# 104 overwritten products in front of one chunk pair: thirteen ways of reading the moving or the stationary side

## The chip, the core and the metric

The kernel runs on one core of one Trainium2 chip. The time is that of the device for one execution, in microseconds (us). The execution before has a median of 1122.11 us over two runs.

## What is computed

A row of 512 tokens with 1024 features goes through two blocks. The first has a gated spatial mix and a causal convolution, the second two kinds of attention. Each ends in a feed-forward part with 4096 hidden features. The pair in question belongs to that of the first block:

```python
h = rms_norm(x, norm2_g[l])
f = jnp.square(jax.nn.relu(jnp.einsum('bsd,df->bsf', h, w_ff1[l])))
x = x + jnp.einsum('bsf,fd->bsd', f, w_ff2[l])
```

All of it is float32 in the reference.

## The kernel before, in words

Activations lie transposed: a tile holds 128 features on the partitions and the 512 tokens along the free dimension. Each float32 matrix is split into a high part, rounded to a format that TensorE takes in one pass (`F32R` in the code, `fp32r` in the profile, though the profile writes a moving side of it as f32), and a low part, the rest. A product is made of three MATMULs: high x high, high x low, low x high (`three()`, lines 749 to 751). `xh` and `xl` are the high and low part of the normalised activations, of shape 128 x 8 x 512; `wh[slot]` and `wl[slot]` are those of a weight chunk of 128 x 1024 in one of four slots.

The weights come as a stream of chunks. Each chunk is loaded by DMA into `raw`, split by GpSimd (lines 548, 551 and 678 to 688 of the profile), and then used by TensorE.

The up-projection of a feed-forward part works on pairs of chunks, and in each pair it saves one product in eight: seven products of half size take the place of eight, with sums of weights and of activations as operands. The tokens are cut in two halves, `EARLY` (0 to 255) and `LATE` (256 to 511). `t_high[0..3]` and `t_low[0..3]`, each 128 x 4 x 256, hold the sums of activations, made once per feed-forward part. The weight sums are made per pair by VectorE (`weight_sums_first`, `weight_sums_last`, `weight_rest`) and ScalarE (`sum_round`). `pair(p)` issues the seven products of pair `p`. Each is a `product(...)`: four tiles of the contraction, three MATMULs of 256 columns each, 12 in all, so a pair is 84. `product_bank(p, i)` is the first half of one of the banks 0 to 4 in turn. VectorE adds the seven results into tiles and signals `part_added` and `evacuated`; ScalarE makes ReLU and square; then the next pair comes. TensorE waits for `split_ready` (GpSimd's split of the chunk), `sum_ready` (the weight sums), `part_added` and `evacuated` (a bank is free).

Four runs of pairs exist. Run 0 has pairs 0 to 3, run 1 pairs 4 to 11; `pairs_of(1)[2]` is pair 6, whose `place_in` is 2, and whose first product goes to bank (7 x 2 + 0) mod 5 = 4. The order on each engine is written out by hand and joined by semaphores. The slots are such that GpSimd splits the chunks of pair p + 1 after products of pair p (`split_pair` waits for `product_done`), and VectorE makes the weight sums of pair p + 1 while it adds the products of pair p.

Every `mm` (`nc.tensor.matmul`) is a load of the stationary side (LDWEIGHTS, engine PEld in the profile) and a MATMUL. `start=True` overwrites what the bank holds.

Of the kernel before, what the change touches and what calls it, by code (L numbers as in the profile page):

```python
# [32 lines left out]
P = 128  # L33
# [28 lines left out]
EARLY = slice(0, Q)  # L62
# [115 lines left out]
def pairs_of(run):  # L178

    first = sum(count for _, _, count in PAIR_RUNS[:run])  # L180
    return range(first, first + PAIR_RUNS[run][2])


def run_of(p):

    return next(run for run in range(len(PAIR_RUNS)) if p in pairs_of(run))


def place_in(p):

    return p - pairs_of(run_of(p))[0]
# [27 lines left out]
def build(nc, a):  # L219
    ctx = ExitStack()  # L220
    with ctx:
# [13 lines left out]
        def sem(name):  # L235
            return ctx.enter_context(nc.semaphore(name))
# [4 lines left out]
        xh = sb("xh", [P, KT, S], F32R)  # L241
# [4 lines left out]
        wh = [sb(f"wh{i}", [P, 1024], F32R) for i in range(SLOTS)]  # L246
        wl_at = place[0]
        wl = [sb(f"wl{i}", [P, 1024], F32R) for i in range(SLOTS)]
# [43 lines left out]
        half = FH // 2 * S * 4  # L292
# [33 lines left out]
        t_high = [at(f"t_high{i}", [P, 4, Q], F32R, o) for i, o in  # L326
                  enumerate((behind, behind + 8192, tmb_at, tmp_at))]
# [15 lines left out]
        bank = [ctx.enter_context(nc.psum_tensor(f"bank{i}", [P, S], F32)) for i in range(8)]  # L343
# [52 lines left out]
        product_done, product_kept, part_added = sem("product_done"), sem("product_kept"), sem("part_added")  # L396
# [348 lines left out]
        def _(pe):  # L745
            mm = nc.tensor.matmul
# [235 lines left out]
            for m in range(4):  # L982
                n = C_U + m
# [104 lines left out]
            def product(out, slot, part, mh, ml):  # L1088

                for k in range(4):  # L1090
                    ks = slice(512 * part + k * P, 512 * part + k * P + P)
                    last = three(out, wh[slot][:, ks], wl[slot][:, ks], mh(k), ml(k), k == 0, k == 3)
                return last

            def pair(p):

                n, run = chunk_of(p), run_of(p)
# [3 lines left out]
                slot = [slot_of(p, role) for role in range(4)]  # L1101

                pe.wait_ge(split_ready, n + 1)
                if alone:
                    pe.wait_ge(evacuated, e - 3)
                    if run == 3:
                        pe.wait_ge(down_out, 16 + TB + 1)
                else:
                    pe.wait_ge(part_added, 5 * p - 3)
                product(out[0], slot[0], 0, lambda k: xh[:, k, EARLY], lambda k: xl[:, k, EARLY]  # L1110
                        ).then_inc(product_done, 1)
                if alone:
# [1870 lines left out]
```

## Time and profile before

| What | Value |
|---|---|
| median of the runs | 1122.11 us |
| span of the profiled execution | 1120.9 us |
| instructions | 17261 |
| TensorE MATMUL busy | 1110.7 us, 6163 instructions |
| TensorE weight load busy | 940.3 us |
| VectorE busy | 704.8 us |
| GpSimd busy | 681.6 us |
| ScalarE busy | 401.7 us |

Times in the profile count from the start of the span. Busy time is the union of the instructions' durations on an engine. Durations of MATMULs overlap, since the next starts before the last has left the array; how fast a row of them goes is read from start to start. A line of the timeline with x4 is four instructions merged, with the time from the first start to the last end. PEclk is the granted clock of TensorE as a share of full speed (2.4 GHz).

### The profile page before, as it was taken

To read this page: it belongs to the slowest core of one execution; us is meant where nothing else is said; L and a number is where in the kernel's file an instruction comes from. 1 tells how busy PE (TensorE), PEld (TensorE's weight loads), DVE (VectorE), ACT (ScalarE), POOL (GpSimd) and SP (SyncE) were. 2 spreads that over 40 slices of the span, in tenths; PEclk is the share of its full clock that TensorE was granted. 3 is DMA by queue.
4 is the path that set the end of the run, shared out by engine and by line. 5 is a ranking of instruction groups with operands and counts; after the bars stand their busy time and mean duration, and the time that the engine had idled before them with its cause. 6 is when DMAs were issued, how large, how long until landed. Compare 5 with 4: busy or idle time off the path is not lost.

```text
span 1120.9 us, 17261 instructions
## 1 busy us (share of the span) xinstructions
PE 1110.7 (99%) x6163; PEld 940.3 (84%) x6163; DVE 704.8 (63%) x1381; ACT 401.7 (36%) x817; POOL 681.6 (61%) x460
## 2 busy tenths in 40 slices
PE   8999999999999999999999999999999999999997
PEld 6888888998889998888778777677899888999886
DVE  5999778850158853547789777666887113885023
ACT  5156566530015531120202346645665000554012
POOL 7879946586636686667456433135847763558662
PEclk9999999999999999999999999999999999999999
DMA  7321222342213342334343221112224822235412
GB/s 253 131 87 64 75 81 89 112 133 94 94 61 111 113 151 96 107 98 132 113 129 98 84 87 58 38 58 75 76 76 138 183 94 69 86 111 179 160 57 75
DMA packets 52251, 115.54 MB, mean 103 GB/s; under 512 B 21840, under 2 KB 22480, under 8 KB 52176
## 3 DMA queue, kind: packets, MB, share of 16 engines
q1 hardware_dynamic: 31200, 105.40, 28.3%
q10 hardware_dynamic: 20976, 9.15, 3.4%
q8 instruction: 46, 0.75, 0.3%
q14 instruction: 29, 0.24, 0.1%
HBM read 105.09 MB, written 4.19 MB: 97 GB/s over the span
## 4 chain that ended last, share of the span: by engine, by line
PE 96%; ACT 1%; DVE 1%; DMA 0%; issue 0%; SPq 0%; ACTq 0%; DVEq 0%
PE bank L749 21%; PE bank L751 20%; PE bank L750 20%; PE bank L1425 5%; PE bank L1427 5%; PE bank L1426 5%; PE bank L781 2%; PE bank L783 2%; PE bank L782 2%; PE bank L1260 2%; PE bank L822 1%; PE bank L1274 1%; PE bank L832 1%; PE bank L823 1%; PE bank L1214 1%; PE bank L1298 1%
## 5 line engine op out<-in xcount | busy, mean ns | idle before, releaser
L551 POOL TENSOR_TENSOR wl<-raw,wh 128x1024 fp32r<-128x1024 f32 x140 | 337.1, 2408 | 11.7
L548 POOL TENSOR_SCALAR wh<-raw 128x1024 fp32r<-128x1024 f32 x139 | 149.1, 1073 | 258.6 <-PE bank L751 144.0
L749 PE MATMUL bank<-xh,wh 128*128 128x512 f32 (+2 forms) x672 | 234.5, 349 | 0.0
L751 PE MATMUL bank<-xh,wl 128*128 128x512 f32 (+2 forms) x672 | 229.4, 341 | 0.0
L750 PE MATMUL bank<-xl,wh 128*128 128x512 f32 (+2 forms) x672 | 229.1, 341 | 0.0
L749 PEld LDWEIGHTS bank<-xh,wh 128*128 128x128 f32 x672 | 126.8, 189 | 29.1 <-issue 16.6
L1659 ACT ACTIVATE wh<-bank 128x512 fp32r<-128x512 f32 x96 | 52.2, 596 | 253.1 <-DVE bank L2338 109.7
L751 PEld LDWEIGHTS bank<-xh,wl 128*128 128x128 f32 x672 | 126.8, 189 | 14.2
L750 PEld LDWEIGHTS bank<-xl,wh 128*128 128x128 f32 x672 | 126.9, 189 | 12.6 <-issue 0.2
L749 PE MATMUL bank<-uh,wh 128*128 128x512 f32 x288 | 112.8, 392 | 0.0
L751 PE MATMUL bank<-uh,wl 128*128 128x512 f32 x288 | 112.1, 389 | 0.0
L750 PE MATMUL bank<-ul,wh 128*128 128x512 f32 x288 | 112.1, 389 | 0.0
L750 PE MATMUL bank<-t_low,wh 128*128 128x256 f32 x384 | 107.6, 280 | 0.0
L751 PE MATMUL bank<-t_high,wl 128*128 128x256 f32 x384 | 107.3, 280 | 0.0
L749 PE MATMUL bank<-t_high,wh 128*128 128x256 f32 x384 | 107.3, 279 | 0.0
L1426 PE MATMUL bank<-wl,uh 128*128 128x512 f32 x240 | 93.4, 389 | 0.0
L1427 PE MATMUL bank<-wh,ul 128*128 128x512 f32 x240 | 93.4, 389 | 0.0
L1425 PE MATMUL bank<-wh,uh 128*128 128x512 f32 x240 | 93.4, 389 | 0.0
L1986 DVE TENSOR_TENSOR bank<-bank,rb 128x512 f32<-128x512 f32 x16 | 11.2, 699 | 111.4 <-PE bank L751 111.4
L2353 DVE TENSOR_TENSOR wl<-bank,wh 128x512 fp32r<-128x512 f32 x96 | 63.2, 682 | 25.5 <-ACT wh L1659 25.0
L685 POOL TENSOR_SCALAR wh<-raw 128x512 fp32r<-128x512 f32 x24 | 14.9, 620 | 102.7 <-PE bank L751 90.0
L749 PEld LDWEIGHTS bank<-t_high,wh 128*128 128x128 f32 x384 | 72.8, 189 | 0.0
(378 smaller groups left out, 2283.2 us busy)
## 6 DMA issues: line engine op xcount, KB each, us to landing
raw<-wstream SPq DMA_DIRECT2D x188, 512.0 KB, 3.5
x<-xT SPq DMA_DIRECT2D x8, 256.0 KB, 4.8
x4rows<-x_rows ACTq DMA_DIRECT2D x4, 512.0 KB, 9.1
out<-x4rows SPq DMA_DIRECT2D x8, 256.0 KB, 2.1
qd<-ropey ACTq DMA_DIRECT2D x16, 64.0 KB, 2.2
kd<-ropey ACTq DMA_DIRECT2D x16, 64.0 KB, 2.1
qa<-ropey SPq DMA_DIRECT2D x16, 64.0 KB, 2.0
ka<-ropey SPq DMA_DIRECT2D x16, 64.0 KB, 2.0
```

Source lines behind the costliest of these rows:

```text
L548: nc.gpsimd.tensor_scalar(wh[c][:], raw[c][:], 1.0, 1.0, ALU.mult, ALU.mult).then_inc(high_ready, 1)
L551: nc.gpsimd.tensor_tensor(wl[c][:], raw[c][:], wh[c][:].bitcast(F32), ALU.subtract).then_inc(split_ready, 1)
L749: mm(out, wh_, mh, start=start, stop=False)
L750: mm(out, wh_, ml, start=False, stop=False)
L751: return mm(out, wl_, mh, start=False, stop=stop)
L781: mm(out, xh[:, k, ts], wh[s][:, ws], start=k == 0, stop=False)
L782: mm(out, xh[:, k, ts], wl[s][:, ws], start=False, stop=False)
L1425: mm(out, uh[:, f, ts], wh[s][:, ws], start=f == 0, stop=False)
L1426: mm(out, uh[:, f, ts], wl[s][:, ws], start=False, stop=False)
L1427: last = mm(out, ul[:, f, ts], wh[s][:, ws], start=False, stop=f == 15)
L1659: A(wh[slot_of(p, role)][:, 512 * part:512 * part + 512], bank[7 - made % 2][:], ACT.Copy).then_inc(sum_rounded, 1)
L2353: V.tensor_tensor(wl[slot][:, at], bank[7 - made % 2][:], wh[slot][:, at].bitcast(F32), ALU.subtract).then_inc(sum_ready, 1)
```

## The change

In front of pair 6, behind the waits of its first product, 104 MATMULs are issued. All write bank 4, each with `start=True` and `stop=True`, and nobody reads the results: product 0 of the pair starts afresh in the same bank. Thirteen ways of reading are gone through, each with k = 0 to 3 and the high and the low weights of the slot, which is eight MATMULs. Twelve ways differ in the moving side: `xh` or `t_high[0]` or `t_high[2]`, 128, 256, 384 or 512 columns, and either side by side or, with `turns(ap, n)`, in turn from n places (the innermost dimension has n elements, one from each n-th part of the tile). `half_tokens` takes 256 columns in turn from the two halves of 512 tokens, 0 to 127 and 256 to 383. The thirteenth reads `xh[:, k, 0:P]` as the moving side and every fourth element of `weights` as the stationary side.

```diff
--- before.py
+++ after.py
@@ -1107,6 +1107,30 @@
                         pe.wait_ge(down_out, 16 + TB + 1)
                 else:
                     pe.wait_ge(part_added, 5 * p - 3)
+                if p == pairs_of(1)[2]:
+                    pe.wait_ge(part_added, 5 * p - 3)
+                    whole = bank[(7 * place_in(p) + run // 3) % 5]
+
+                    def turns(ap, n):
+                        return ap.rearrange("p (half n) -> p n half", half=n)
+
+                    def half_tokens(ap):
+                        return ap.rearrange("p (half n) -> p n half", half=2)[:, 0:P]
+
+                    for moves in (lambda k: xh[:, k, EARLY], lambda k: turns(xh[:, k, EARLY], 2),
+                                  lambda k: half_tokens(xh[:, k]), lambda k: turns(xh[:, k, EARLY], 4),
+                                  lambda k: t_high[0][:, k], lambda k: turns(t_high[0][:, k], 2),
+                                  lambda k: turns(t_high[2][:, k], 2), lambda k: turns(xh[:, k], 2),
+                                  lambda k: turns(xh[:, k], 4), lambda k: turns(xh[:, k, P:], 2),
+                                  lambda k: xh[:, k, 0:P], lambda k: turns(xh[:, k, 0:P], 2)):
+                        for k in range(4):
+                            for weights in (wh[slot[0]], wl[slot[0]]):
+                                moved = moves(k)
+                                columns = int(np.prod(moved.shape[1:]))
+                                mm(whole[:, 0:columns], weights[:, k * P:k * P + P], moved, start=True, stop=True)
+                    for k in range(4):
+                        for weights in (wh[slot[0]], wl[slot[0]]):
+                            mm(whole[:, 0:P], weights[:, k:k + 4 * P:4], xh[:, k, 0:P], start=True, stop=True)
                 product(out[0], slot[0], 0, lambda k: xh[:, k, EARLY], lambda k: xl[:, k, EARLY]
                         ).then_inc(product_done, 1)
                 if alone:
```

## Rows read from the trace of the kernel before

**Rows 1.** The page: span, busy times of TensorE, its tenths, granted clock, chain.
```profile
span 1120.9 us, 17261 instructions
...
PE 1110.7 (99%) x6163; PEld 940.3 (84%) x6163; DVE 704.8 (63%) x1381; ACT 401.7 (36%) x817; POOL 681.6 (61%) x460
...
PEclk9999999999999999999999999999999999999999
...
PE 96%; ACT 1%; DVE 1%; DMA 0%; issue 0%; SPq 0%; ACTq 0%; DVEq 0%
```

**Rows 2.** Waits of TensorE, all; us in total, times, longest.
```profile
PE bank L969 <- DVE tmp L2040: 1.5, 1, 1.5
PE bank L945 <- DVE xl L2005: 1.0, 2, 0.5
PE bank L888 <- DVE rn L2034: 0.6, 1, 0.6
PE bank L822 <- issue: 0.2, 1, 0.2
```

**Rows 3.** Timeline of TensorE: first products of pairs 6 and 7, last of 5.
```profile
345.08 0.28 PE L751 MATMUL bank<-t_high,wl 128*128 128x256 f32 x1
345.19 0.28 PE L749 MATMUL bank<-xh,wh 128*128 128x256 f32 x1
...
355.10 0.28 PE L749 MATMUL bank<-xh,wh 128*128 128x256 f32 x1
```

**Rows 4.** Windows: span, busy of PE, PEld, DVE, ACT, POOL, clock, DMA, GB/s.
```profile
345.19:355.10 9.91, 9.91 (x86) 9.91 (x85) 8.72 (x18) 5.76 (x11) 5.98 (x5) 1.00 0.29 107
129.60:130.50 0.90, 0.90 (x4) 0.41 (x3) 0.69 (x2) 0.90 (x1) 0.90 (x1) 1.00 0.00 0
645.00:655.00 10.00, 10.00 (x60) 8.33 (x59) 6.58 (x23) 3.04 (x10) 3.43 (x2) 1.00 0.24 76
```

**Rows 5.** Waits of all engines in pair 6, the longest four.
```profile
ACT wh L1659 <- DVE bank L2345: 3.2, 1, 3.2
POOL wh L685 <- PE bank L751: 2.9, 1, 2.9
ACT wh L1659 <- DVE bank L2338: 0.9, 1, 0.9
POOL wh L678 <- PE bank L751: 0.9, 1, 0.9
...
```

**Rows 6.** Timeline of TensorE: steps of 512 and of 384 columns.
```profile
404.67 0.39 PE L749 MATMUL bank<-uh,wh 128*128 128x512 f32 x1
...
411.94 0.39 PE L751 MATMUL bank<-uh,wl 128*128 128x512 f32 x1
...
516.10 0.33 PE L749 MATMUL bank<-xh,wh 128*128 128x384 f32 x1
...
516.45 0.34 PE L751 MATMUL bank<-xh,wl 128*128 128x384 f32 x1
```

**Rows 7.** Timeline and groups of TensorE: plain f32 products, transposes, single columns.
```profile
129.61 1.02 PE L902 MATMUL bank<-conv_p,center 128*128 128x512 f32 x2
...
636.77 0.60 PE L1274 MATMUL bank<-ident,probs 128*128 128x128 f32 x4
...
647.26 1.03 PE L866 MATMUL bank<-inv,sq 128*128 128x1 f32 x8
...
L1274 PE MATMUL bank<-ident,probs 128*128 128x128 f32 x120 | 18.6, 274 | 0.0
...
L866 PE MATMUL bank<-inv,sq x32: 250/250/251, 647.3 to 694.7; 128*128 128x1 f32 x32
...
L902 PE MATMUL bank<-conv_p,center x2: 590/590/591, 129.6 to 130.0; 128*128 128x512 f32 x2
```

**Rows 8.** Groups of VectorE and GpSimd (line engine op names shapes xcount | busy us, mean ns).
```profile
L2344 DVE TENSOR_TENSOR bank<-raw,bank 128x512 f32<-128x512 f32 x24 | 16.5, 686 | 0.1
...
L551 POOL TENSOR_TENSOR wl<-raw,wh 128x1024 fp32r<-128x1024 f32 x140 | 337.1, 2408 | 11.7
```

## The prediction

> **What bounds the kernel now.** I read the page's busy shares first, then the waits of TensorE, then the one pair of chunks in front of which the new products go. TensorE is busy for 1110.7 of the 1120.9 us of the span, the granted clock stands at nine tenths or more in every slice, and 96% of the chain that ended last is TensorE's [rows 1]. Its waits in the whole execution sum to 3.3 us [rows 2]. So TensorE sets the end, and nothing that stands idle on it can soak up added work.
>
> The edit sits in `pair(p)` for `p == pairs_of(1)[2]`, which is pair 6: the third of the eight pairs of run 1. A pair is 84 products of 256 columns, and pair 6 goes from 345.19 to 355.10 us [rows 3]. There TensorE is busy for all 9.91 us at full granted clock, the 2.4 GHz level; VectorE is busy for 8.72, GpSimd for 5.98 and ScalarE for 5.76 [rows 4]. The waits of that stretch are all those of other engines; the longest four: GpSimd waits 2.9 and 0.9 us for TensorE's products, ScalarE 4.1 us for VectorE [rows 5]. The view lists none of TensorE, so the 3.3 us lie elsewhere. Whatever time the new products take is put in series in front of pair 6.
>
> **The change part by part.** It removes nothing, moves nothing, issues no DMA. It adds one wait, for `part_added` at 27, which is the wait that already stands two lines above it (`5 * p - 3`): its price is nothing, since the same count has just been passed. What is queued behind it is all of TensorE's work, and none of it comes later for the wait. It adds 104 MATMULs, each with its weight load. All write bank 4 and start afresh; product 0 of pair 6 starts afresh in the same bank, after them on the same engine. The other engines hold no work that could move ahead: for pair 6 they are done, and for pair 7 they wait for signals that pair 6 gives after the new products. When TensorE resumes, each of those distances is as before, so I look for no gain behind it and no second loss: 0, cover none.
>
> So the question is only how fast the 104 run. By columns they are: 16 of 256 that lie side by side (`xh` EARLY and `t_high[0]`); 40 of 256 that jump (five ways); 16 of 512 that jump (two ways); 8 of 384 that jump; 8 of 128 side by side; 8 of 128 that jump; 8 of 128 side by side whose stationary side is read with a step of four elements. "Jump" means that the innermost dimension has two or four elements 64 to 256 elements apart, so no column lies beside the one before it.
>
> *Side by side.* Durations in the groups overlap (a product of 256 columns has a mean of 279 to 282 ns), so I price by start to start. The pair gives 9.91 us / 84 = 0.118 us for 256 columns [rows 3]. For 512 columns, 404.67 to 411.94 us, the first products of the down-projection, is 32 steps, 0.227 us each [rows 6]; for 384, 516.10 to 516.45, with one between, is two steps of 0.175 us [rows 6].
>
> *128 columns.* No product of this number format has 128 columns in the trace. Plain f32 transposes of 128 columns, four in a row, take 0.60 us in all and 0.27 us for one: (0.60 - 0.27) / 3 = 0.110 us a step. Eight sums with a moving side of a single column take 1.03 us with 0.25 for one: (1.03 - 0.25) / 7 = 0.111 us [rows 7]. One column costs as much as 128, so it is the weight load of 128 columns that sets this step, about 0.87 ns per stationary column. I take 0.111 us for all 24 products of 128 columns. The lower end, if this format's loads are faster, is the column rate plus the change-over: 0.118 x 128 / 256 + half of a change-over is about 0.065 us.
>
> *Jumping columns.* The trace has no jumping moving side. Two rates at which TensorE takes a moving side are in it: full (0.227 us / 512 = 0.44 ns per column, above) and half. The plain f32 product at 129.61 us has two instructions of 512 columns; together 1.02 us with 0.59 for one, so 1.02 - 0.59 = 0.43 us a step or 0.84 ns per column [rows 7], at a granted clock that is full in the same stretch [rows 4]. The weight load's 0.87 ns per column is the same again. I read this as TensorE's fetch: where each column needs a fetch of its own it gets one per 0.84 ns, and neighbours share one. That is an inference and both ends stay: below, the full rate; above, the nearest rates of other engines that take one element per step: VectorE 686 ns / 512 = 1.34 ns and GpSimd 2408 ns / 1024 = 2.35 ns [rows 8]. I take 0.84 ns, the row of TensorE itself. With 0 to 12 ns of change-over (0.118 less 256 / 2.4 GHz is 11 ns) 256 columns are 0.215 to 0.227, taken as 0.22 us; 512 are 0.43 to 0.44, taken as 0.435; 384 are 0.323 to 0.335, taken as 0.327.
>
> The Trainium skill, page "Advanced Engine Details and Errata", section "Memory Cachelines", speaks against this change: the on-chip memory is read in lines of 16 bytes, an access keeps full speed only if at least two fall into one line, and one line per access costs a penalty. It gives no size. By that rule the sum would be that of the jumping rates and not that of the full ones. No run shown here bears it out yet. For the stationary side with its step of 16 bytes the same rule asks for a penalty too.
>
> *The stationary side with a step of four.* Its load already takes the slow 0.87 ns per column with columns side by side, so one fetch per column changes nothing: 0.111. If it doubles, 8 x 0.11 = 0.9 us more.
>
> *The sum.*
> 16 x 0.118 = 1.9; 40 x 0.22 = 8.8; 16 x 0.435 = 7.0; 8 x 0.327 = 2.6; 24 x 0.111 = 2.7. In all 23.0 us. The span would go from 1120.9 to 1143.9 us. The median of the runs is 1122.1, 1.2 us above the profiled span, and goes to 1145.1. With the change-over ends and the 128-column lower end (-0.4 to -1.1), and a doubled strided load (+0.9), this case covers 1144.0 to 1146.5 us.
>
> **The rivals.**
>
> *Jumping costs nothing.* TensorE could hold several open fetches, above all where only two places alternate. For it: the fetch is not seen to bind in any row. The price: 56 x 0.118 + 16 x 0.227 + 8 x 0.175 + 24 x 0.111 = 6.6 + 3.6 + 1.4 + 2.7 = 14.3 us, so 1136.4 us, 1.3% over and thus within 2%; 1135.3 with the short 128-column step. It decides the sign of the verdict: 2% is 22.4 us, which my sum passes by 0.6 us only. If even one of the 512-column ways (8 x 0.21 = 1.7 us) runs at the full rate, the total is under it. Mixed cases (two places free, four places slow, or some distances slow) lie between 1136 and 1145.
>
> *Jumping costs more than one step per column.* Two fetches to the same part of memory might have to follow each other. For it: the other engines' rates. Against: those rates belong to engines with clocks and pipes of their own. The jumping columns number 40 x 256 + 16 x 512 + 8 x 384 + 8 x 128 = 22528. At 1.34 ns they take 30.2 us; with 16 x 0.118 and 16 x 0.111 beside them the sum is 33.9 us: 1156.0 us. At 2.35 ns it is 56.6 us: 1178.7 us.
>
> *The clock falls.* A TensorE that is fed at half rate for some 18 us could be granted 1.2 GHz. The stretches of plain f32 and single-column work show full clock at 129 and at 645 us [rows 4], and in the latter they stand between dense products, so it isn't excluded. If everything in the insert took twice its time, that is 46 us: 1168 us.
>
> *It doesn't do what it says.* The products are overwritten, so something might drop them: 1122.1 us. Nothing in the kernel's way of naming each instruction speaks for it.
>
> **How the numbers follow.** Half rate for all jumping ways 0.45; full or mixed 0.28; more than one step per column 0.22; clock 0.03; dropped or some gain 0.02. The likeliest gives 1145.1 us, with 1144.0 to 1146.5 as its own range. The range to be held 8 times in 10 takes in the full rate with its low end (1135) and, above, the 1.34 ns case (1157); left out are the rates above it, the fallen clock and the dropped products, some 0.15. By 2% (about what a measurement of this kernel can tell from no change), the half rate splits: 0.28 above and 0.17 within. Slower: 0.28 + 0.22 + 0.03 = 0.53, and 0.54 with the mixed cases' tail. Same: 0.17 + 0.27 + 0.01 = 0.45. Faster: 0.01.
>
> **What would show it.** In the profile after, the last product of pair 5 (a `t_high` product at 345.08 us) should be followed by 104 products on bank 4 in steps of 0.118 for `xh` EARLY and `t_high[0]`, 0.22 for the five jumping ways of 256, 0.43 for the two of 512, 0.33 for 384 and 0.11 for each way of 128, and pair 6 should begin near 368.2 us and still take 9.91 us. Steps of 0.118 in the jumping ways show the first rival, steps over 0.3 the second. A granted clock under 1 shows the third. Different steps for different distances would break my single rate; a TensorE wait inside or behind the insert would break the claim that all of it is in series and nothing more.

## The result, and the profile after

The change takes 1138.26 us in the median of two runs (1137.74 to 1138.77) where the kernel before takes 1122.11: the ratio is 1.0143, with a 95% interval of 1.0124 to 1.0162. The second set of runs, below, gave 1138.27 and 1.0144. It is slower beyond doubt and by less than 2%. The likeliest case of the prediction, 1145.1 us with 1144.0 to 1146.5 as its own range, did not come true; the time lies between it and the first rival (1136.4 us), inside the wide range of 1135 to 1157 us.

The page of the kernel after, span and busy times, answers to [rows 1]:

```profile
span 1136.0 us, 17469 instructions
...
PE 1126.6 (99%) x6267; PEld 955.0 (84%) x6267; DVE 702.9 (62%) x1381; ACT 402.1 (35%) x817; POOL 683.3 (60%) x460
```

All 104 products are there (6267 less 6163). TensorE's busy time grew by 15.9 us, the span by 15.1; VectorE's fell by 1.9 and GpSimd's grew by 1.7.

The windows of the kernel after (columns as in [rows 4]: span of the window, busy of PE, PEld, DVE, ACT and POOL, granted clock, DMA share, GB/s), first the insert, then pair 6:

```profile
344.71:360.17 15.46, 15.46 (x106) 14.52 (x105) 3.24 (x7) 1.09 (x2) 1.91 (x2) 1.00 0.18 68
360.17:370.15 9.98, 9.98 (x85) 9.98 (x86) 6.17 (x11) 4.80 (x9) 4.04 (x3) 1.00 0.01 2
```

The insert takes 15.46 us at full granted clock. While it runs, the other engines finish what they had and stop: VectorE is busy for 3.24 of the 15.46 us. Pair 6 takes 9.98 us where it took 9.91, and most of that is its first step, 0.17 us in place of 0.12. It is no mark of the slow loads of the thirteenth way: the first step is 0.17 us too behind products of 128 columns whose weights lie side by side (all side by side and the thirteenth way alone, below). The other way about, the step from the first product of 128 columns behind wider ones to the second is 0.06 us, and the next are 0.111. The down-projection, which began at 404.67 us [rows 6], begins at 419.72, 15.05 us later. The missing 0.4 us lies ahead of the insert: it starts at 344.71 us, where pair 6 began at 345.19 before, and TensorE's waits at line 945 are 0.2 us in place of 1.0 [rows 2]. The view of the waits has none of TensorE between 340 and 380 us. So the cost is in series, at one place, and nothing is given back behind it.

The timeline of TensorE in the kernel after: the first product of each of the thirteen ways, in their order in the code, then the first of pair 6. Each way has eight products, so the distance to the next line is eight steps.

```profile
344.71 0.28 PE L1130 MATMUL bank<-xh,wh 128*128 128x256 f32 x1
...
345.65 0.28 PE L1130 MATMUL bank<-xh,wh 128*128 128x256 f32 x1
...
346.54 0.28 PE L1130 MATMUL bank<-xh,wh 128*128 128x256 f32 x1
...
347.44 0.30 PE L1130 MATMUL bank<-xh,wh 128*128 128x256 f32 x1
...
348.54 0.28 PE L1130 MATMUL bank<-t_high,wh 128*128 128x256 f32 x1
...
349.49 0.27 PE L1130 MATMUL bank<-t_high,wh 128*128 128x256 f32 x1
...
350.38 0.28 PE L1130 MATMUL bank<-t_high,wh 128*128 128x256 f32 x1
...
351.27 0.38 PE L1130 MATMUL bank<-xh,wh 128*128 128x512 f32 x1
...
353.00 0.45 PE L1130 MATMUL bank<-xh,wh 128*128 128x512 f32 x1
...
355.26 0.33 PE L1130 MATMUL bank<-xh,wh 128*128 128x384 f32 x1
...
356.57 0.23 PE L1130 MATMUL bank<-xh,wh 128*128 128x128 f32 x1
...
357.41 0.27 PE L1130 MATMUL bank<-xh,wh 128*128 128x128 f32 x1
...
358.30 0.40 PE L1133 MATMUL bank<-xh,wh 128*128 128x128 f32 x1
...
360.17 0.34 PE L749 MATMUL bank<-xh,wh 128*128 128x256 f32 x1
```

Worked out from these lines, beside what the prediction took:

| Way | Columns | Step after, us | Predicted, us |
|---|---|---|---|
| 1 `xh` side by side | 256 | 0.118 | 0.118 |
| 2 two places, 128 apart | 256 | 0.111 | 0.22 |
| 3 two places, 256 apart | 256 | 0.113 | 0.22 |
| 4 four places, 64 apart | 256 | 0.138 | 0.22 |
| 5 `t_high[0]` side by side | 256 | 0.119 | 0.118 |
| 6, 7 two places, 128 apart | 256 | 0.111 | 0.22 |
| 8 two places, 256 apart | 512 | 0.216 | 0.435 |
| 9 four places, 128 apart | 512 | 0.283 | 0.435 |
| 10 two places, 192 apart | 384 | 0.164 | 0.327 |
| 11 side by side | 128 | 0.105 | 0.111 |
| 12 two places, 64 apart | 128 | 0.111 | 0.111 |
| 13 stationary side with a step of four | 128 | 0.234 | 0.111 |

Three things stand out. Reading in turn from two places is not dearer than side by side, it is cheaper (0.216 against 0.227 us for 512 columns). Four places cost about 1.2 times side by side (0.138 against 0.118 us, 0.283 against 0.227). And the stationary side, whose step of four was thought free, takes twice its time. Two entries need care. The 0.105 of way 11 is a mean with the short first step of 0.06 in it; behind the first the step is 0.111, as in way 12. And ways 2, 6 and 7 take with 256 columns what way 12 takes with 128, 0.111 us, so there it may be the load and not the reads that sets the step.

### The profile page after: what moved, and what is told of

It is laid out like the page before. It is cut to its first block, busy times and chain, and to the rows that moved or that the text cites. A ratio compares the mean times of both kernels' runs of the same rounds, so it can differ in the third digit from the quotient of the medians.

```text
span 1136.0 us, 17469 instructions
## 1 busy us (share of the span) xinstructions
PE 1126.6 (99%) x6267; PEld 955.0 (84%) x6267; DVE 702.9 (62%) x1381; ACT 402.1 (35%) x817; POOL 683.3 (60%) x460
## 4 chain that ended last, share of the span: by engine, by line
PE 96%; ACT 1%; DVE 1%; DMA 0%; issue 0%; SPq 0%; ACTq 0%; DVEq 0%
PE bank L749 21%; PE bank L751 20%; PE bank L750 20%; PE bank L1449 5%; PE bank L1451 5%; PE bank L1450 5%; PE bank L781 2%; PE bank L782 2%; PE bank L783 2%; PE bank L1284 2%; PE bank L1130 1%; PE bank L822 1%; PE bank L1298 1%; PE bank L832 1%; PE bank L823 1%; PE bank L1238 1%
## 5 line engine op out<-in xcount | busy, mean ns | idle before, releaser
L751 PEld LDWEIGHTS bank<-xh,wl 128*128 128x128 f32 x672 | 126.8, 189 | 14.3
```

The source lines that it names most:

```text
L751: return mm(out, wl_, mh, start=False, stop=stop)
```

## The experiments

All but two put another insert at the same place, behind the same wait, in front of pair 6, and leave the rest of the kernel before as it is. The steps below are all worked out from the first starts of one way and the next.

**All side by side.** Is it the way of reading, or the place in the row of 104? The same counts and columns, with no jump and no step:

```diff
+  mm(whole[:, 0:256], w[:, k * P:k * P + P], xh[:, k, EARLY], start=True, stop=True)
...
+  mm(whole[:, 0:P], w[:, k * P:k * P + P], xh[:, k, 0:P], start=True, stop=True)
```

> The same 104 products in front of the same pair with the same numbers of columns, all read side by side, on the stationary side too. Theory 1 (jumping from two places is not dearer than side by side; only four places in turn and the stationary step of four are): 56 x 0.118 + 16 x 0.227 + 8 x 0.173 + 24 x 0.107 = 14.2 us for the insert, 1.3 us less than the change's 15.46. The parts behind that: the two four-place ways give back 8 x (0.1375 - 0.118) + 8 x (0.2825 - 0.227) = 0.6 us, the stationary way 8 x (0.234 - 0.107) = 1.0 us, and the six two-place ways cost 0.3 us more. Theory 2 (the steps of a way hang on its place in the row, what runs beside it or what came before, and not on how it is read): the seventh to tenth way keep their steps of 0.22 to 0.28 and 0.16 us at other places than their columns explain, and the insert stays at 15.5 us. Time over the kernel before: 14 to 15 us by theory 1, 16 us by theory 2.

Measured: 1136.97 us, 14.5 over the kernel before in the same set (ratio 1.0129, 1.0112 to 1.0146). The insert's first line and that of pair 6 behind it, in the timeline of this kernel:

```profile
344.51 0.28 PE L1120 MATMUL bank<-xh,wh 128*128 128x256 f32 x1
...
358.84 0.33 PE L749 MATMUL bank<-xh,wh 128*128 128x256 f32 x1
```

That is 14.33 us, 1.13 less than in the change, where theory 1 said 1.3; the steps are 0.114 to 0.120, 0.226 to 0.229, 0.176 and 0.105 to 0.113 us (with 256 columns 0.120 in most ways, 0.114 in the one that reads `t_high[2]`). This is what the first rival priced at 14.3 us. Where a step was slow in the change it is not at the same place here, so theory 2 falls.

**The change once more**, since 16.15 us by the runs and 15.46 by the trace don't match.

> The change itself once more. Its two earlier times lie 1.0 us apart and 16.15 us over the kernel before in the middle, where the insert in the trace is 15.46 us long and the span grew by 15.1. Theory 1 (only the insert's length counts): the median comes to 15.1 to 15.6 us over the kernel before and the 16.15 was scatter. Theory 2 (about a microsecond is lost elsewhere): it stays at 16 us or more, and the profile shows a stage that is longer.

Measured: 1138.27 us (1137.85 to 1139.41), 15.9 over the kernel before (1122.41). Its span is 1136.1 us, 15.2 over that of [rows 1], and the insert is 15.46 us again (344.88 to 360.34). Neither theory fits as it stands: the median is 0.3 us above what theory 1 allows, and no stage shows the microsecond of theory 2. Part of the gap is which execution the profile shows. The time of an execution is 1.7 us more than its span in each of the listed ones; the profiled one is the fastest of its four (1137.85), while the spans of the other three are 1136.3, 1136.8 and 1137.7, and the profile of the kernel before, 1120.9 us, lies near the top of the 1120.1 to 1121.0 of its thirteen. Median against median the growth is 15.9 us, 0.4 above the insert's length. That is less than the scatter of the four times (1.6 us), and it stays open.

**The thirteenth way alone made side by side.**

```diff
-  mm(whole[:, 0:P], weights[:, k:k + 4 * P:4], xh[:, k, 0:P], start=True, stop=True)
+  mm(whole[:, 0:P], weights[:, k * P:k * P + P], xh[:, k, 0:P], start=True, stop=True)
```

> The change with the thirteenth way alone made side by side: its eight products load 128 neighbouring weights. Theory 1 (a load with a step of four elements takes 0.234 us, one side by side 0.106): the insert goes from 15.46 to 14.4 us, 8 x 0.128 = 1.0 us less, and the first product behind it follows after 0.11 us instead of 0.17. Theory 2 (the last eight are slow for their place in front of the pair): they stay at 0.23.

Measured: 1136.99 us, 1.3 less than the change in the same set. The timeline of this kernel, the first of the eight and the first of pair 6:

```profile
358.58 0.28 PE L1133 MATMUL bank<-xh,wh 128*128 128x128 f32 x1
...
359.48 0.33 PE L749 MATMUL bank<-xh,wh 128*128 128x256 f32 x1
```

Eight steps of 0.113 us in place of 0.234: the eight are slow because of how they read, and they hold 1.0 us of the cost (the insert is 14.49 us). In one point theory 1 missed: the first step of pair 6 behind the insert is still 0.17 us, not 0.11.

**Thirteen ways of reading the moving side.** How does the cost go with places and steps? Three of the thirteen (`flat` is `xh` with its eight tiles as one row; the weights are 128 side by side):

```diff
+  mm(whole[:], w[:, k % 4 * P:k % 4 * P + P], turns(xh[:, k], 8), start=True, stop=True)
...
+  mm(whole[:], w[:, k % 4 * P:k % 4 * P + P], xh[:, k].rearrange("p (half n two) -> p n half two", half=2, two=2), start=True, stop=True)
...
+  mm(whole[:], w[:, k % 4 * P:k % 4 * P + P], flat[:, k:k + 1024:2], start=True, stop=True)
```

> Instead of the 104 products stand thirteen other ways of reading the moving side, 14 or 16 products each, weights side by side: 512 columns side by side; in turn from 2, 4, 8 and 16 places; 384 columns from 6 places; two neighbours at a time from 2 and from 4 places; two runs of 256 one after the other; and with a constant step of 2, 3, 4 and 8 elements. Theory 1 (the number of places in turn decides): 0.227 side by side, 0.216 for 2 places, 0.28 for 4, and more, up to 0.43, for 8 and 16; neighbours in twos from 2 places 0.216; constant steps behave as one place, 0.22 each up to a step of 3 and dearer from 4 on, where each column has 16 bytes of its own. Theory 2 (how many columns share a piece of 16 bytes decides): 2 places should then have been dear too, which they were not, unless pieces are kept; 8 and 16 places equal 4 places at 0.28, and a constant step of 4 and of 8 costs 0.28 too. Theory 3 (distance decides): 16 places, 32 elements apart, differ from 8, 64 apart, in no steady order.

The timeline of this kernel, the first product of 2, 4, 8 and 16 places and of what follows, then of the constant steps of 2 and 3; each way is 16 products:

```profile
349.12 0.38 PE L1123 MATMUL bank<-xh,wh 128*128 128x512 f32 x1
...
352.57 0.43 PE L1126 MATMUL bank<-xh,wh 128*128 128x512 f32 x1
...
357.09 0.68 PE L1129 MATMUL bank<-xh,wh 128*128 128x512 f32 x1
...
364.87 0.64 PE L1132 MATMUL bank<-xh,wh 128*128 128x512 f32 x1
...
371.84 0.41 PE L1135 MATMUL bank<-xh,wh 128*128 128x384 f32 x1
...
391.27 0.61 PE L1147 MATMUL bank<-xh,wh 128*128 128x512 f32 x1
...
398.49 0.64 PE L1150 MATMUL bank<-xh,wh 128*128 128x512 f32 x1
```

Two places 0.216, four 0.283, eight 0.486, sixteen 0.436 us a step; a constant step of two elements 0.451. Further, from the same view: side by side 0.228, 384 columns from six places 0.237, neighbours in twos from two places 0.333 and from four 0.444, two runs of 256 one after the other 0.230, steps of 3, 4 and 8 elements 0.451, 0.461 and 0.432. So the half rate of the prediction exists, at 0.84 to 0.95 ns per column, but it belongs to constant steps and to many places. Theory 1 missed, as it wanted steps of 2 and 3 at 0.22 and neighbours in twos at 0.216, and so did theory 2, which wanted eight places at 0.28. Theory 3 (distance) is left open by this run; the run on distance settles it. Reading at half rate did not touch the clock, as the window of the steps of 2 and 3 shows (granted clock in the third column from the end):

```profile
391.00:405.00 14.00, 14.00 (x33) 6.58 (x33) 0.00 (x0) 0.00 (x0) 0.00 (x0) 1.00 0.00 0
```

**Why side by side costs more than two places.**

```diff
+  mm(whole[:], w[:, 0:P], xh[:, k], start=True, stop=True)
...
+  mm(whole[:], w[:, k % 4 * P:k % 4 * P + P], flat[:, k * 512 + 4:k * 512 + 516], start=True, stop=True)
...
+  mm(in_pairs(whole[:], 2), w[:, k % 4 * P:k % 4 * P + P], in_pairs(xh[:, k], 2), start=True, stop=True)
```

> Why do 512 columns side by side take 0.227 us a step and from two places in turn 0.216? Fourteen or sixteen products each: side by side; the same with one and the same weights throughout; weights with a step of 2; weights with a step of 4 and two places in turn; side by side starting 1, 4 and 32 elements later; the stationary side from xh as well; output written in pairs of neighbours to two places in turn, with the moving side side by side, and with it in the same pairs; the moving side alone in pairs; last two places in turn. Theory 1 (the load of the weights and the moving side get in each other's way when both walk through memory one after the other): other starts and another stationary side change the 0.227, a step of 2 in the weights too. Theory 2 (it is the order of the reads of the moving side itself): all side-by-side ways stay at 0.227 and pairs from two places are 0.216. Theory 3 (the pattern with two dimensions as such is faster): pairs are 0.216 too. If output in pairs costs nothing, the last but two way has the same 0.216 and gives the result in the usual order, which would make a faster kernel; if the accumulator's memory minds, it is above 0.227.

Steps: side by side 0.228; with the same weights throughout 0.227; with `xh` on the stationary side 0.228; weights with a step of 2 0.233; weights with a step of 4 and two places in turn 0.236; starts 1, 4 and 32 elements later 0.238, 0.232 and 0.234; output alone in pairs to two places 0.226; moving side and output in pairs 0.339, moving side alone in pairs 0.340; two places 0.216. Other weights side by side change nothing, nor does the order of the output, and a pattern of more dimensions is not faster as such. Theory 2 stands in this, that the order of the moving side's reads decides; its 0.216 for pairs was wrong, and so was its claim that all side-by-side ways stay at 0.227: other starts add 2 to 5%, a step of 2 in the weights 2%, and no run shows why.

**Distance, or who keeps what.** From these steps I formed theory L: even and odd columns go two separate ways, and a way is fast as long as its next column lies in the 16 bytes it holds. It was written down with a number for each of thirteen ways, some of them new. Three of these:

```diff
+  mm(whole[:], w[:, k % 4 * P:k % 4 * P + P], xh[:, k].rearrange("p (g h n) -> p g n h", h=2, n=4), start=True, stop=True)
...
+  mm(whole[:], w[:, k % 4 * P:k % 4 * P + P], xh[:, k:k + 2, 0:S:2].rearrange("p t n -> p n t"), start=True, stop=True)
...
+  mm(whole[:], w[:, k % 4 * P:k % 4 * P + P], flat.rearrange("p (n e) -> p n e", e=8)[:, 32 * k:32 * k + 256, 0:2], start=True, stop=True)
```

> Thirteen more ways of reading the moving side, 14 or 16 products each, 512 columns except where said, weights side by side. In order: side by side; in turn from two places 256 elements apart; from two places 512 apart; from two places 4 apart (order 0 4 1 5 2 6 3 7); from two places 2 apart (0 2 1 3); from two places 512 apart, every second element of each; from two places 2048 apart, every fourth element of each; two neighbours out of every eight; four neighbours out of every eight; in turn from four places 1024 apart; from eight places 512 apart; four neighbours at a time from two places 256 apart; side by side again. Theory L (even and odd columns go two separate ways, and each way is fast as long as its next column lies in the 16 bytes it holds): 0.227; 0.216; 0.216; 0.216; 0.22; 0.227, for each way finds two columns in 16 bytes; 0.43 to 0.46; 0.43 to 0.46; 0.227; 0.281; 0.43 to 0.49; 0.227 or a little more; 0.227. Theory D (distance and the part of memory that it hits): two places 4 and 2 elements apart are slow, 0.43, and four places 1024 apart and eight 512 apart differ from the 0.281 and 0.4875 at 128 and 64 elements. Theory S (columns in one piece of 16 bytes, two are enough): two neighbours out of eight run at 0.227, every second element of two places at 0.43.

The timeline of this kernel, from its fourth way on, in order: two places 4 apart; two places 2 apart; every second element of two places 512 apart; every fourth of two places 2048 apart; two neighbours out of every eight; four neighbours out of every eight; four places 1024 apart; eight places 512 apart; four neighbours at a time from two places:

```profile
355.33 0.38 PE L1129 MATMUL bank<-xh,wh 128*128 128x512 f32 x1
...
358.78 0.39 PE L1132 MATMUL bank<-xh,wh 128*128 128x512 f32 x1
...
362.42 0.39 PE L1135 MATMUL bank<-xh,wh 128*128 128x512 f32 x1
...
365.60 0.61 PE L1138 MATMUL bank<-xh,wh 128*128 128x512 f32 x1
...
372.84 0.64 PE L1141 MATMUL bank<-xh,wh 128*128 128x512 f32 x1
...
379.28 0.41 PE L1144 MATMUL bank<-xh,wh 128*128 128x512 f32 x1
...
383.00 0.44 PE L1147 MATMUL bank<-xh,wh 128*128 128x512 f32 x1
...
387.50 0.68 PE L1150 MATMUL bank<-xh,wh 128*128 128x512 f32 x1
...
395.29 0.45 PE L1153 MATMUL bank<-xh,wh 128*128 128x512 f32 x1
```

With 16 products a way (14 in the third and fifth), the steps are 0.216, 0.228, 0.227, 0.453, 0.460, 0.233, 0.281 and 0.487 us; four neighbours at a time from two places take 0.252. Theory L wrote 0.216, 0.22, 0.227, 0.43 to 0.46, 0.43 to 0.46, 0.227, 0.281, 0.43 to 0.49 and 0.227 "or a little more"; the last is 11% more, the largest miss. Distance as such does not matter: two places 4, 256 or 512 elements apart are alike, four places 128 or 1024 apart too. Theory D falls with that. Theory S falls with two neighbours out of eight, which have two columns in one piece and still run at half rate. The rows sort by how many of the even columns (0, 2, 4 and so on) come in a row from one piece of 16 bytes, and the odd ones likewise. Four: 0.216 (two places 4, 256 or 512 apart). Two: 0.227 to 0.233 (side by side, two places 2 apart, every second element of two places, four neighbours out of eight). One, and then a new piece: 0.43 to 0.46 (constant steps, every fourth element of two places, two neighbours out of eight). That is what theory L says, and it fits these rows; that the chip has two separate ways is inferred from them and not seen. What theory L does not explain is the size of the steps between full and half rate: why a way that goes back and forth between two pieces pays 0.28 us from four places and 0.34 us in pairs, and why eight places are slower than sixteen. That stays open.

**Ways of reading the stationary side.**

```diff
+  mm(whole[:, 0:P], w[:, k:k + 2 * P:2], xh[:, k, 0:P], start=True, stop=True)
...
+  mm(whole[:], w[:, k:k + 4 * P:4], xh[:, k], start=True, stop=True)
...
+  mm(whole[:, 0:32], w[:, k % 4 * P:k % 4 * P + P], xh[:, k, 0:32], start=True, stop=True)
```

> Ways of reading the stationary side, 16 products each, with 128 moving columns: side by side and with a step of 2, 3, 4, 7 and 5 elements; then 128 and 256 moving columns in turn from two places; then 256 and 512 moving columns side by side, each with a stationary side side by side and with a step of 4; last 32 moving columns. Theory 1 (a column that has 16 bytes of its own takes two steps of loading): step 2 costs 0.11 as side by side does, step 3 lies between, 4, 5 and 7 cost 0.234 alike; with 256 moving columns the load of step 4 still sets the step (0.234), with 512 it nearly hides (0.23 to 0.25). Theory 2 (any step but one turns a fast load off): 2 and 3 cost 0.234 as well. Theory 3 (the cost goes with the distance): 7 costs more than 4. With 32 columns side by side the step stays at 0.11 if the load sets it.

With 128 moving columns: side by side 0.108, step 2 0.119, step 3 0.176, step 4 0.234 us. With 32 moving columns, side by side, 0.106. Both side-by-side means hold a short first step, 0.06 and 0.03 us; behind the first both step at 0.111. So it is the load that sets the step of small products, as the prediction read from single columns [rows 7]. A load with a step of 4 takes 0.234 beside 256 moving columns as well, and beside 512 it is all but hidden, 0.234 against 0.229. So a slow load costs only what it exceeds the product beside it. The ways between can't be read as they stand, as the windows of this kernel show (granted clock in the third column from the end):

```profile
348.30:351.10 2.80, 2.80 (x18) 2.80 (x18) 0.01 (x1) 0.00 (x0) 0.00 (x0) 1.00 0.74 265
351.10:354.90 3.80, 3.80 (x18) 3.80 (x18) 0.00 (x0) 0.00 (x0) 0.00 (x0) 0.82 0.01 3
354.90:358.60 3.70, 3.70 (x18) 3.70 (x17) 0.00 (x0) 0.00 (x0) 0.00 (x0) 0.50 0.00 0
...
369.10:371.70 2.60, 2.60 (x18) 2.60 (x17) 0.00 (x0) 0.00 (x0) 0.00 (x0) 0.71 0.00 0
371.70:375.40 3.70, 3.70 (x18) 3.70 (x17) 0.00 (x0) 0.00 (x0) 0.00 (x0) 1.00 0.00 0
```

TensorE was granted the 1.2 GHz level from among the loads with a step of four on, and the 2.4 GHz level again from among products of 256 columns side by side; the loads with a step of four beside 256 columns, right behind (3.7 us), ran at 2.4 GHz. Steps of 7 and 5 elements took 0.231 and 0.224 us there, hardly other than step 4, most of which ran at 2.4 GHz; but 128 columns from two places took 0.213 where way 12 of the change took 0.111.

**Is it the slow loads that bring the clock down?** Two inserts of 128 products of 128 columns each, alike but for the reading of the stationary side: side by side in the first, with a step of four in the second. Each ran once.

```diff
+  mm(whole[:, 0:P], w[:, k % 4 * P:k % 4 * P + P], xh[:, k % 8, 0:P], start=True, stop=True)
...
+  mm(whole[:, 0:P], w[:, k % 8:k % 8 + 4 * P:4], xh[:, k % 8, 0:P], start=True, stop=True)
```

> The insert is 128 products of 128 columns, moving and stationary side side by side, in place of the 104. In the run with thirteen ways of reading the stationary side the granted clock fell to half some 9 us after the insert began, among products whose load had a step of four or more. Theory 1 (the slow loads, 128 columns in 0.234 us, leave TensorE too little to do): here, with 128 columns in 0.108 us, the clock stays at 1.00 for all 13.8 us, and the time grows by about 14 us. Theory 2 (any long row of products of 128 columns does it): the clock falls to half here too, the step goes from 0.108 to 0.213 us behind the fall, and the time grows by 18 us or more.

Measured: 1136.49 us, 14.1 over the kernel before in the same set; the insert goes from 344.64 to 358.88 us, 0.111 us a step, with a granted clock of 1.00 throughout.

> The same 128 products, with a step of four elements in the stationary side: 128 x 0.234 = 30 us. Theory 1: the clock falls to half some 5 to 10 us into the insert and stays there; the steps stay at 0.22 to 0.24 us, since it is the reads of the load and not the array that set them; behind the insert the first products of the pair take 0.22 us a step in place of 0.118 until the clock is back, as after the other run's fall, which adds 2 to 5 us: the time grows by 32 to 35 us. Theory 2: the same with the fall at the same place. If the clock stays at 1.00, the fall in the other run came from elsewhere.

Measured: 1153.9 us, 31.5 over the kernel before. The windows of this kernel, the last two behind the insert, which goes from 345.05 to 374.92 us:

```profile
348.00:350.00 2.00, 2.00 (x10) 2.00 (x10) 0.70 (x2) 0.00 (x0) 0.00 (x0) 1.00 0.92 352
350.00:352.00 2.00, 2.00 (x10) 2.00 (x10) 0.00 (x0) 0.00 (x0) 0.00 (x0) 0.76 0.27 109
352.00:354.00 2.00, 2.00 (x10) 2.00 (x10) 0.00 (x0) 0.00 (x0) 0.00 (x0) 0.50 0.00 0
...
376.00:378.00 2.00, 2.00 (x11) 2.00 (x11) 0.00 (x0) 0.17 (x1) 0.00 (x0) 0.50 0.00 0
378.00:380.00 2.00, 2.00 (x18) 2.00 (x17) 0.08 (x1) 1.97 (x5) 0.32 (x1) 0.92 0.00 0
```

The clock fell 6 us into the slow loads and not at all beside the quick ones. So it is the slow loads that bring it down and not a long row of products of 128 columns. What it is about them, the "too little to do" of theory 1, no run separates. The loads' own step stayed at 0.23 to 0.24 us at either level. What pays for the clock is the work behind: the first 15 products of pair 6 take 3.31 us (0.32 the first, 0.21 to 0.22 each of the others) in place of 15 x 0.118, 1.5 us more, so the total is just under the 32 to 35 us expected.

**A use of it: the moving side read from two places.** If two places are 5% faster than side by side, the kernel itself can be read so. `uh` and `ul` of the first block are stored as even tokens, then odd tokens, and the down-projection reads them in turn.

```diff
-  A(uh[:, f % FH], pair_buffer(p, i), ACT.Square).then_inc(uh_ready, 1)
+  A(turns(uh[:, f % FH]), in_twos(pair_buffer(p, i)), ACT.Square).then_inc(uh_ready, 1)
-  V.tensor_tensor(ul[:, f % FH], src, uh[:, f % FH].bitcast(F32), ALU.subtract)
+  V.tensor_tensor(turns(ul[:, f % FH]), in_twos(src), turns(uh[:, f % FH]).bitcast(F32), ALU.subtract)
```

> No insert. The kernel before, with uh and ul of the first block's feed-forward part stored as even tokens first and odd tokens behind (ScalarE and VectorE write them so), and read in turn from the two halves by the down-projection, which gives the usual order of tokens in the result. The 864 products of 512 columns of the three lines with uh and ul come down from 0.227 to 0.216 us a step if the read from two places is what is faster: 864 x 0.011 = 9.5 us less than the kernel before, 1112.9 us, about 0.85%. If writing with a step makes ScalarE or VectorE slow (they are busy for 5.8 and 8.7 of the 9.9 us of a pair), the pairs wait for them and the gain is less, or turns into a loss. If 0.216 was due to the overwriting products only, no gain.

Measured: 1122.6 us, ratio 1.0004 (0.9994 to 1.0014): no difference. The two down-projections came down from 87.5 and 87.1 us to 83.4 and 83.0, 0.217 us a step and 8.2 us in all. (The expectation counted 864 products; they are 768.) The pairs took it back: run 0 grew from 39.7 to 42.2 us, run 1 from 79.3 to 85.4. Two groups of this kernel in the window of pair 6, VectorE's and ScalarE's writes of `ul` and `uh`, and then TensorE's longest wait from the view of its waits:

```profile
L2413 DVE TENSOR_TENSOR ul<-bank,uh 128x512 fp32r<-128x512 f32 x2 | 2.3, 1136 | 1.3 <-ACT bank L1692 1.3
...
L1684 ACT ACTIVATE uh<-ss 128x512 fp32r<-128x512 f32 x1 | 1.2, 1171 | 0.0
```

```profile
PE bank L755 <- DVE ss L2402: 1.6, 1, 1.6
```

The operations that write `uh` and `ul` to two places take 1171 and 1136 ns where they took 632 and 685 (that of VectorE also reads `uh` from two places). VectorE had 8.7 of 9.9 us [rows 4]; now it has 0.9 us more per pair, and ScalarE 1.1. Run 1 shows the lag building up: its first four pairs keep 9.9 us, the next three take 10.95, 11.05 and 11.04, the last 12.7. Pair 6 and the sixth pair of the run in the windows of this kernel:

```profile
343.26:353.18 9.92, 9.92 (x87) 9.92 (x85) 8.19 (x16) 6.83 (x11) 5.53 (x5) 1.00 0.30 107
374.04:385.09 11.05, 10.77 (x85) 10.22 (x85) 9.33 (x18) 6.77 (x12) 5.51 (x5) 1.00 0.28 97
```

VectorE isn't busy all the time in the long pair either (9.33 of 11.05 us, 1.3 of the rest in a wait for ScalarE). So the bound is the chain that goes through VectorE and ScalarE; that follows from the waits and the longer operations, and no run makes one of the two quick again.

**The same with no scattered write.** The order of tokens is set once, when `xh`, `xl` and the activation sums are made, by reads with a step of four; products in the pairs then read from two places too.

```diff
-  A(xh[:, k], x1_bank[k % 4][:], ACT.Copy, scale=col("norm2", k)).then_inc(xh_ready, 1)
+  A(laid(xh[:, k]), taken(x1_bank[k % 4][:]), ACT.Copy, scale=col("norm2", k)).then_inc(xh_ready, 1)
...
+  order = turns if first_block[0] else lambda ap: ap
-  last = three(out, wh[slot][:, ks], wl[slot][:, ks], mh(k), ml(k), k == 0, k == 3)
+  last = three(out, wh[slot][:, ks], wl[slot][:, ks], order(mh(k)), order(ml(k)), k == 0, k == 3)
```

> No insert. In the first block's feed-forward part every moving side is read in turn from two places, and ScalarE and VectorE do nothing more in the pairs than before. xh and xl are stored once with token 4j + 2g + h at place 256h + 128g + j, and the sums of activations t_high and t_low follow the same order; each product of 256 columns reads in turn from two places 128 apart, the plain chunks do so in each half, and the results come out as even tokens, then odd tokens. The down-projection reads those in turn from two places 256 apart and gives the usual order. Only the 8 tiles of xh and xl and the activation sums are made from reads with a step (VectorE makes each xl tile in two instructions). Theory L: 768 products of 512 columns of the down-projections save 0.011 us each, 8.2 us as the last run showed; 1008 products of 256 in the pairs save 0.007 each, 7.0 us; 192 of 512 in the plain chunks save 2.1 us: 17 us less than the kernel before, 1105 us, if VectorE keeps up with pairs of 9.3 us in place of 9.9, of which it is busy for 8.7. The rival: VectorE's chain through a pair (sums of weights, seven results, two rests) is longer than 9.3 us with its waits, and the pairs keep 9.9 us; then 8 to 10 us are saved, 1113 us. If the reads with a step slow the making of xh and xl, where TensorE takes each tile as it comes, some of it is lost at the start of the part.

Measured: 1112.11 us against 1122.34, ratio 0.991 (0.9893 to 0.9926): 10.2 us faster than the kernel before. The timeline of this kernel, beginning of run 1, of the second down-projection, and of what follows it:

```profile
320.81 0.27 PE L764 MATMUL bank<-xh,wh 128*128 128x256 f32 x1
...
398.01 0.48 PE L764 MATMUL bank<-uh,wh 128*128 128x512 f32 x1 [0.92 <-DVE ss L2429]
...
481.00 0.40 PE L764 MATMUL bank<-xh,wh 128*128 128x512 f32 x1
```

The second down-projection takes 82.99 us (87.06 before), run 1 77.20 (79.32), run 0 39.34 (39.66), the first down-projection 83.32 (87.53). That is 10.7 us of span. The 8 us of the down-projections arrived whole, of the 7 us in the pairs only 2.4, of the 2 us in the plain chunks none. The rival of this run came nearest with its 8 to 10 us, but its reason holds only in part, for the pairs did not keep 9.9 us. In run 1 the first five take 9.38 us each, 0.112 us a step, the next two 9.67 and 9.77, the last 10.86. One of the five in the windows of this kernel:

```profile
339.57:348.95 9.38, 9.38 (x86) 9.38 (x85) 8.19 (x16) 5.75 (x11) 5.47 (x5) 1.00 0.31 113
```

And TensorE has three waits that the kernel before doesn't have, 4.2 us in all: 1.7 for VectorE in the plain chunks, 1.6 for ScalarE in the first pair of run 0, 0.9 for VectorE behind run 1.

## Why the prediction was right or wrong

**All of it in series, nothing given back: right.** The insert of 15.46 us moved the next down-projection by 15.05 us and the span by 15.1, and the difference lies ahead of the insert. The waits of the other engines in the pair made no difference.

**Side by side: right.** 16 products at 0.118 were priced at 1.9 us and took 1.89. The price from start to start, not from the durations of 279 to 282 ns, is what made that so.

**128 columns are set by the load: right** for the two ways with weights side by side (0.111 us a step behind the first), and shown by 32 columns, which step at 0.111 too. The Trainium skill, page "TensorE: Matmul & The Clock Gate", section "LDWEIGHTS (loading the stationary operand)", puts a load at the number of its columns by 1.2 GHz, which is 107 ns for 128. The runs agree within 4 ns for weights side by side (0.111 us) and not for a step of three or four (0.176 and 0.234).

**One rate of 0.84 ns for every jumping column: wrong, and the step that failed.** It stood in for 40 x 0.22, 16 x 0.435 and 8 x 0.327, 18.4 us. Measured, they are 4.67, 3.99 and 1.31 us, 10.0 in all, so 8.4 us too much. The reading behind it, one fetch per column unless the columns are neighbours, took the reads as one stream in order. The runs show that it is not neighbourhood that counts: two neighbours out of every eight run at 0.460 us, two places in turn, with no neighbours at all, at 0.216. What fits the rows is that columns 2i and 2i + 2 have to be near each other (in one piece of 16 bytes), not 2i and 2i + 1. Two places in turn keep that, and keep it better than side by side does. The half rate itself is real (0.432 to 0.46 us for steps of 2, 3, 4 and 8), and the row of TensorE that it came from [rows 7] was the right size, for patterns that this change doesn't contain.

**The step of four in the stationary side at no cost: wrong, the other way.** The text kept a doubling as an upper end, 0.9 us; it was 8 x 0.123 = 1.0 us. The argument was that the load already took its slow rate. It takes that rate with columns side by side, and there is a slower one.

**The rule on lines of 16 bytes.** The Trainium skill, page "Advanced Engine Details and Errata", section "Memory Cachelines", wants at least two accesses to one line of 16 bytes for full speed. The stationary side agrees, nearly (0.111 us side by side, 0.119 with a step of two, 0.176 with three, 0.234 with four). On the moving side it does not decide: a step of two elements has two columns in 16 bytes and runs at 0.451 us, and two places in turn change the line with each column and run at 0.216. By that rule, too, the prediction came to the sum of the jumping rates, which the change did not take; on the stationary side the rule was right, and the prediction set it aside.

**The first rival**, jumping costs nothing, was the nearest: 14.3 us against 15.46, the rest being the two four-place ways (0.6 us), the stationary way (1.0 us) and the two-place ways, which gave 0.3 to 0.4 back. The "mixed" case named just this, between 1136 and 1145 us, and shared its chance of 0.28; to give one rate for all ways 0.45 was too much, where not one row showed any of them. **More than one step per column** did not occur: the most in any way tried was 0.487 us for eight places, 0.95 ns per column, where the rival's lower case had 1.34. **The clock** stayed at 1.00 in the change. The rival feared a moving side at half rate, and the run on moving sides answers it: 28.7 us in a row with steps of 2, 3, 4 and 8 elements (391.27 to 420.00 us), at 1.00. What did lower the clock was a row of 128 slow loads; the change has eight of them.

**The range and the verdict by 2%.** The time lies in the range because the range reached down to the first rival, not because the mechanism was right: the likeliest case missed by 6.8 us. The prediction gave slower by over 2% 0.54 and within 2% 0.45. It was within 2%.

## What to carry to other kernels

Price a row of products from start to start, and price the moving and the stationary side apart: the slower of the two sets the step, and a load of 128 weights (0.11 us side by side, 0.23 with a step of four) shows only beside products that are shorter than it (up to 256 columns here). A moving side read in turn from two places costs no more than side by side, 5% less in this kernel with 512 columns, while a constant step of two already halves the rate. Before a faster read is bought with a scattered write, look at the engine that writes: here the same idea gave nothing with the write scattered inside the pairs and 10 us with the order set once ahead of them.

## What the runs showed of the hardware that was not expected

- Two places in turn: 0.216 us for 512 columns and 0.164 for 384, so 0.41 ns for one column more, which is one cycle of 2.4 GHz. 512 cycles are 213 ns; beside them stand 3 ns, and 14 where the columns lie side by side (0.227 us).
- Half rate on the moving side (0.43 to 0.49 us for 512 columns) for constant steps of 2 and more, for two neighbours out of every eight, and for eight and sixteen places, all at full granted clock; four places 0.28 us at any distance tried (128 and 1024 elements).
- Output written in pairs of neighbours to two places of a bank costs nothing (0.226 us).
- In a row of 128 slow loads (0.234 us each) the granted clock fell to the 1.2 GHz level 6 us after the first, although TensorE was busy all the time, and it was back at 2.4 GHz 3.4 us into the work behind (374.92 to about 378.3 us). 28.7 us of moving sides at half rate left it at 1.00. The loads themselves took 0.23 to 0.24 us at either level.
- ScalarE and VectorE take 1.9 and 1.7 times as long to write 512 elements in turn to two places (1171 for 632 ns; 1136 for 685, where VectorE reads one input in turn too).
